# FFN 2's gate and up by 2x2 blocks with seven products, with one weight sum made in memory

## The reference

```
h = modulate(rms_norm(x, norm_ffn2), shift3, scale3)              # 512 x 1024
x = x + 0.5 * g3 * ((silu(h @ w_gate) * (h @ w_up)) @ w_down)     # w_gate, w_up: 1024 x 2816
```

## Time and profile before

| | |
|---|---|
| median of 3 runs | 1163.62 us (1163.49 to 1168.38) |
| the profiled execution | 1163.01 us |
| its span in the profile | 1161.2 us |
| mean granted clock of PE | 0.997 |
| PE busy | 1145.9 us, 99% of the span |
| DVE, ACT, POOL busy | 625.5, 451.7, 58.9 us |
| FFN 2's gate and up loop | 811.8 to 1029.4 us |

### The profile page before, as it was taken

How to read it: one execution, slowest core, us unless ns; L and a number is a source line. 1 busy time by engine, 2 the same in 40 slices (tenths; PEclk the granted TensorE clock), 3 DMA queues, 4 the chain that set the end, 5 groups by cost and what they waited for, 6 DMA issues and landing times.

```text
span 1161.2 us, 16214 instructions
## 1 busy us (share of the span) xinstructions
PE 1145.9 (99%) x5730; PEld 969.9 (84%) x5730; DVE 625.5 (54%) x1051; ACT 451.7 (39%) x709; POOL 58.9 (5%) x86
## 2 busy tenths in 40 slices
PE   8899999999999999999999999999999999999997
PEld 7788888888888998888888888899888888888887
DVE  5766666666555666776565566756433333333332
ACT  5233332332222357665555566434322222222232
POOL 3301000000000000010001010000000000000000
PEclk9999999999999999999999999999999999999999
DMA  9567566556555423343343442341333333333332
GB/s 312 162 219 243 181 218 204 174 184 211 172 172 167 110 63 102 91 125 86 90 120 96 111 117 72 91 139 37 97 98 101 90 98 101 90 93 94 99 113 74
DMA packets 221149, 151.45 MB, mean 130 GB/s; under 512 B 5078, under 2 KB 202916, under 8 KB 221108
## 3 DMA queue, kind: packets, MB, share of 16 engines
q1 hardware_dynamic: 217108, 138.76, 39.8%
q0 software_dynamic: 3280, 9.79, 3.2%
q10 hardware_dynamic: 720, 2.36, 0.6%
HBM read 148.73 MB, written 4.52 MB: 132 GB/s over the span
## 4 chain that ended last, share of the span: by engine, by line
PE 91%; DVE 2%; SPq 2%; issue 1%; DMA 1%; ACT 1%; POOL 0%; DVEq 0%; POOLq 0%; ACTq 0%
PE bank L1492 28%; PE bank L1494 28%; PE bank L1493 28%; PE bank L1827 2%; PE bank L1820 1%; SPq L446 1%; PE bank L1843 1%; PE bank L1815 1%; PE bank L1842 1%; DMA raw<-in_ffn_w_gate_dram 1%; SPq L465 1%; DMA adas<-in_ada_w_dram 1%; SPq L459 0%; DVE hL L1010 0%; DVE tmp L1005 0%
## 5 line engine op out<-in xcount | busy, mean ns | idle before, releaser
L1492 PE MATMUL bank<-hH,wH 128*128 128x512 f32 (+1 forms) x1072 | 413.2, 385 | 3.6 <-DVE hL L1010 3.1
L1494 PE MATMUL bank<-hH,wL 128*128 128x512 f32 (+1 forms) x1072 | 409.0, 382 | 0.0
L1493 PE MATMUL bank<-hL,wH 128*128 128x512 f32 (+1 forms) x1072 | 408.8, 381 | 0.0
L617 ACT ACTIVATE wH<-raw 128x1024 fp32r<-128x1024 f32 (+1 forms) x169 | 176.2, 1042 | 500.2 <-PE bank L1494 500.2
L944 DVE TENSOR_TENSOR wL<-raw,wH 128x1024 fp32r<-128x1024 f32 (+1 forms) x169 | 203.4, 1204 | 280.3 <-ACT wH L617 279.7
L1492 PEld LDWEIGHTS bank<-hH,wH 128*128 128x128 f32 x1072 | 201.6, 188 | 44.4 <-issue 5.1
L1494 PEld LDWEIGHTS bank<-hH,wL 128*128 128x128 f32 x1072 | 201.5, 188 | 39.1
L1493 PEld LDWEIGHTS bank<-hL,wH 128*128 128x128 f32 x1072 | 201.8, 188 | 37.7
L1492 PE MATMUL bank<-actH,wH 128*128 128x512 f32 (+1 forms) x332 | 126.9, 382 | 0.0
L1494 PE MATMUL bank<-actH,wL 128*128 128x512 f32 (+1 forms) x332 | 126.6, 381 | 0.0
L1493 PE MATMUL bank<-actL,wH 128*128 128x512 f32 (+1 forms) x332 | 126.6, 381 | 0.0
(11 more groups left out here) (204 smaller groups left out, 1188.6 us busy)
## 6 DMA issues: line engine op xcount, KB each, us to landing
adaw<-in_ada_w_dram SPq DMA_DIRECT2D x28, 1024.0 KB, 6.0
raw<-in_ffn_w_gate_dram SPq DMA_DIRECT2D x43, 512.0 KB, 3.8
raw<-in_ffn_w_up_dram SPq DMA_DIRECT2D x43, 512.0 KB, 3.8
raw<-in_mix_w_in_dram SPq DMA_DIRECT2D x41, 512.0 KB, 3.8
raw<-in_ffn_w_down_dram SPq DMA_DIRECT2D x32, 512.0 KB, 3.7
adas<-in_ada_w_dram SPq DMA_DIRECT2D x16, 512.0 KB, 8.2
raw<-in_ffn_w_down_dram SPq DMA_DIRECT2D x16, 384.0 KB, 3.4
raw<-in_mix_w_out_dram SPq DMA_DIRECT2D x8, 512.0 KB, 3.7
```

The costliest lines, as they stand in the source:

```text
L617: nc.scalar.activation(wH[s][:, :n * P], raw[s][:, :n * P], ACT.Copy).then_inc(hi_done, 1)
L1492: T.matmul(o, a[0], b[0], start=start, stop=False)
L1493: T.matmul(o, a[0], b[1], start=False, stop=False)
L1494: return T.matmul(o, a[1], b[0], start=False, stop=stop)
```

## The change

FF tiles are paired i with i + 11 (`HF` = 11). Pairs 0 and 1 are computed as before (eight units, the last four behind `to_ffn`). Pairs 2 to 10, nine of them, are computed as 2x2 blocks: the depth is cut into its two halves of 512 channels, the columns into tile i and tile i + 11, the tokens into two halves of 256. Such a product of 2x2 blocks takes seven block products in place of eight, each of a sum of weight blocks and a sum of token blocks. One product is 2 matrices x 4 depth tiles x 3 = 24 matmuls of 256 columns; gate and up stand side by side in one bank. The order of the products is 1, 2, 5, 6, 7, 3, 4.

- **Token sums**, once: POOL adds high and low halves of four blocks of h back together (`whole`), DVE makes four sums of them (`token_sums`), and ACT and DVE split these into high and low halves (`t_high`, `t_low`) for products 6, 7, 4 and 5. Products 1, 2 and 3 take blocks of h itself.
- **Weight sums**, for each pair: products 1, 2 and 4 take raw weights. Product 5's sum lies ready in memory (`wsum_d`): POOL issues eight transfers from memory to memory while FFN 1's down runs, and eight that add, one behind each pair's biases in the mixing (704 KB each). DVE makes the others: to 5's sum it adds 1's raw weights in place for 6 and then 2's for 3 (`next_r`), and 1's to the loaded block for 7 (`next_q`).
- **Loads**: five per pair in place of four, each two transfers of 256 KB, into four raw slots used in turn. A slot is free when the last sum or low half that reads it is done.
- **Weight halves**: seven per pair (`w_high` on ACT, `w_low` on DVE) with three slots, two products ahead of PE.
- **Results**: ACT copies the banks of products 1 and 5 out, DVE makes seven sums of 128x512 (`block`); ACT takes Silu of the gate's half, DVE multiplies (`multiply`), ACT and DVE split as before, for two tiles at once.
- **Down**: its first two units' weights go into the token sums' place, and SP loads them after the last `w_low`; the first unit waits for the tiles of eight pairs, the second for all 22.
- The stage is written out on all engines and not in a loop. Three semaphores of the table are merged to one (`table_moved`).

The diff, cut to its core:

```diff
+    ORDER_P = (1, 2, 5, 6, 7, 3, 4)
+    B_P = {1: 4, 2: 7, 5: 5, 6: 6, 7: 0, 3: 1, 4: 2}
...
+    LOADS = (1, 2, 5, 7, 4)
+    PACKET, SUM_ROWS = 4 * P, D // 2 // P
+    N_LOAD, W_SLOTS, RAW_SLOTS = len(LOADS), 3, 4
...
+        def load_of(n):
+            t, p = n // N_BL, ORDER_P[n % N_BL]
+            return N_LOAD * t + LOADS.index(5 if p in (6, 3) else p)
...
+                if l < 2:
+                    sp.wait_ge(lo_done, U_DN2 - 1 + l + FREE)
+                elif l == 2:
+                    sp.wait_ge(t_lo, 3)
+                elif l >= RAW_SLOTS:
+                    t0, p0 = (l - RAW_SLOTS) // N_LOAD, LOADS[(l - RAW_SLOTS) % N_LOAD]
+                    if p0 in (1, 2):
+                        sp.wait_ge(r_made, 2 * t0 + p0)
+                    if p0 == 1:
+                        sp.wait_ge(q_made, t0 + 1)
+                    elif p0 != 2:
+                        sp.wait_ge(w_lo, N_BL * t0 + ORDER_P.index(3 if p0 == 5 else p0) + 1)
+                for m in range(2):
+                    if p == 5:
+                        src = wsum_d[m].rearrange("(k p) n -> p k n", p=P)[:, :, i * P:(i + 1) * P]
+                    else:
+                        k0, tile = {1: (0, i), 2: (DT // 2, i), 4: (DT // 2, i + HF), 7: (0, i + HF)}[p]
+                        src = tiles_of(ws[m], slice(tile * P, (tile + 1) * P), DT // 2, k0)
+                    sp.dma_start(raw_slot(l)[:, m, :].rearrange("p (k n) -> p k n", k=DT // 2), src
+                                 ).then_inc(w_in[l % RAW_SLOTS], 16)
+            for i in range(DT // 2):
+                for k in range(6):
+                    k0, n = PARTS[k % 3]
+                    if i == 0 and k < 2:
+                        sp.wait_ge(w_lo, N_PROD)
+                    t = 2 * i + k // 3
+                    sp_load(sp, U_DN2, 6, i, k, tiles_of(ffn2_w_down, slice(t * P, (t + 1) * P), n, k0))
...
+            def weight_sum(step):
+                kind, row = step // SUM_ROWS, step % SUM_ROWS * P
+                m = kind % 2
+                w = (ffn2_w_gate, ffn2_w_up)[m]
+                to = wsum_d[m, row:row + P, :]
+                if kind < 2:
+                    pool.dma_start(to, w[0, row:row + P, HF * P:], max_dma_last_dim=PACKET).then_inc(w_summed, 16)
+                else:
+                    pool.wait_ge(w_summed, 16 * 2 * SUM_ROWS)
+                    pool.dma_start(to, w[0, D // 2 + row:D // 2 + row + P, HF * P:], accum_op=ALU.add,
+                                   max_dma_last_dim=PACKET).then_inc(w_summed, 16)
...
+            def w_high(n):
+                l, p = load_of(n), ORDER_P[n % N_BL]
+                if p in (6, 3):
+                    act.wait_ge(r_made, 2 * (n // N_BL) + 1 + (p == 3))
+                elif p == 7:
+                    act.wait_ge(q_made, n // N_BL + 1)
+                else:
+                    act.wait_ge(w_in[l % RAW_SLOTS], 32 * (l // RAW_SLOTS + 1))
+                if n < 2:
+                    act.wait_ge(unit_done, U_DN2 - 1 + n)
+                elif n >= W_SLOTS:
+                    act.wait_ge(p_done, n - W_SLOTS + 1)
+                nc.scalar.activation(by_two(w_slot(n)[0]), raw_slot(l), ACT.Copy).then_inc(w_hi, 1)
...
+            def two_by_blocks(t):
+                for at in range(N_BL):
+                    n = N_BL * t + at
+                    if n + 2 < N_PROD:
+                        w_high(n + 2)
+                    else:
+                        k = n + 2 - N_PROD
+                        act.wait_ge(p_done, N_PROD - N_BL + 4 + k)
+                        prep_home(U_DN2 + k, U_DN2)
+                    if t and at == 1:
+                        gates(t - 1, 1)
+                    if t and at in (2, 3):
+                        act_high(t - 1, at - 2)
+                    if at == 1:
+                        act.wait_ge(p_done, n)
+                        if t:
+                            act.wait_ge(multiplied, 2 * t - 1)
+                        nc.scalar.activation(K_P1, bank[:, B_P[1], :], ACT.Copy).then_inc(kept, 1)
+                    if at == 3:
+                        act.wait_ge(p_done, n)
+                        if t:
+                            act.wait_ge(multiplied, 2 * t)
+                        nc.scalar.activation(K_P5, bank[:, B_P[5], :], ACT.Copy).then_inc(kept, 1)
+                    if at == 6:
+                        gates(t, 0)
...
+            def next_r(t, q):
+                n, r = N_BL * t + 2 + q, raw_slot(N_LOAD * t + 2)
+                dve.wait_ge(w_lo, n + 1)
+                V.tensor_tensor(r, r, raw_slot(N_LOAD * t + q), ALU.add).then_inc(r_made, 1)
+            def next_q(t):
+                l = N_LOAD * t + LOADS.index(7)
+                dve.wait_ge(w_in[l % RAW_SLOTS], 32 * (l // RAW_SLOTS + 1))
+                V.tensor_tensor(raw_slot(l), raw_slot(l), raw_slot(N_LOAD * t), ALU.add).then_inc(q_made, 1)
...
+            def block(t, step):
+                to, a, b, copies, made, products = (
+                    (K_U2, K_P1, bank[:, B_P[6], :], 1, 0, 4), (K_P1, K_P1, bank[:, B_P[2], :], 1, 1, 2),
+                    (K_U3, K_U2, bank[:, B_P[7], :], 1, 1, 5), (K_U2, K_U2, K_P5, 2, 3, 0),
+                    (K_U2, K_U2, bank[:, B_P[3], :], 2, 4, 6), (K_P5, K_U3, K_P5, 2, 4, 0),
+                    (K_U3, K_U3, bank[:, B_P[4], :], 2, 6, 7))[step]
...
+            def two_by_blocks(t):
+                for at in range(N_BL):
+                    n = N_BL * t + at
+                    if n + 2 < N_PROD:
+                        w_low(n + 2)
+                    else:
+                        prep_home(U_DN2 + n + 2 - N_PROD)
+                    if at < 2:
+                        next_r(t, at)
+                    if at == 1:
+                        next_q(t)
+                    if t and at == 0:
+                        block(t - 1, 6)
+                        multiply(t - 1, 0)
+                    if t and at == 2:
+                        multiply(t - 1, 1)
+                        act_low(t - 1, 0)
+                    if t and at == 3:
+                        act_low(t - 1, 1)
+                    for step in {4: (0, 1), 5: (2, 3), 6: (4, 5)}[at] if at >= 4 else ():
+                        block(t, step)
...
+            def gate_up_by_blocks():
+                u0 = U_GU2
...
+                for n in range(N_PROD):
+                    t, p = n // N_BL, ORDER_P[n % N_BL]
+                    if t and p in (1, 5):
+                        pe.wait_ge(kept, 2 * t - 1 + p // 5)
+                    elif t:
+                        pe.wait_ge(c_made, 7 * t - 7 + {6: 1, 2: 2, 7: 3, 3: 5, 4: 7}[p])
+                    elif p in (7, 4):
+                        pe.wait_ge(silu_done[1][B_P[p] // 2], DIRECT + START)
+                    elif p == 3:
+                        pe.wait_ge(prod_done[1][0], DIRECT + START)
+                    if t == 0 and p in (5, 6, 7, 4):
...
                         pe.wait_ge(lo_done, u + 1 + FREE)
```

More of the change, by code:

```diff
@@ L348, in hybrid_block @@
         out_sent = sem("out_sent")
+        w_summed = sem("w_summed")
+        w_in = [sem(f"w_in{q}") for q in range(RAW_SLOTS)]
+        r_made = sem("r_made")
+        q_made = sem("q_made")
+        w_hi = sem("w_hi")
+        w_lo = sem("w_lo")
+        p_done = sem("p_done")
+        h_whole = sem("h_whole")
+        t_sum = sem("t_sum")
+        t_hi = sem("t_hi")
+        t_lo = sem("t_lo")
+        kept = sem("kept")
+        c_made = sem("c_made")
+        gated = sem("gated")
+        multiplied = sem("multiplied")
         def head_rows(h):
@@ L585, in _ @@
                     pool.dma_start(modrows, mod_d.rearrange("a (r n) -> (a r) n", n=P)).then_inc(modrows_in, 16)
+                    for step in range(2 * SUM_ROWS):
+                        pool.wait_ge(unit_done, U_DN1 + 2 + 2 * step)
+                        weight_sum(step)
                 if n == 2:
@@ L599, in _ @@
                         biases_a(i)
+                        weight_sum(2 * SUM_ROWS + PAIRS - 1 + i)
+                    weight_sum(2 * SUM_ROWS + 2 * PAIRS - 1)
+                if n == 4:
+                    pool.wait_ge(hL_done, 5 * DT)
+                    for q in range(4):
+                        whole(q)
         @block.scalar
@@ new lines, in t_high, with act_high, gates @@
+            def t_high(p, sums):
+                act.wait_ge(t_sum, sums)
+                nc.scalar.activation(moving(p)[0], hB[{6: 22, 7: 12, 4: 21, 5: 11}[p]][:, :, :], ACT.Copy).then_inc(t_hi, 1)
+            def act_high(t, j):
+                act.wait_ge(multiplied, 2 * t + 1 + j)
+                nc.scalar.activation(actH[:, DIRECT + t + HF * j, :], sg[:, j, :], ACT.Copy).then_inc(actH_done[1], 1)
+            def gates(t, j):
+                act.wait_ge(c_made, 7 * t + (5, 7)[j])
+                act.wait_ge(actL_done[1], 2 * (DIRECT + t) + START)
+                nc.scalar.activation(by_halves(sg[:, j, :]), of_gate((c1, c2)[j]), ACT.Silu, scale=(1.0, -1.0)[j]).then_inc(gated, 1)
```

(82 more changed lines are left out.)

154 lines of the change are left out of this document (136 added, 18 removed).

## The result

The changed kernel takes 1167.4 us in the median of 20 runs (1165.0 to 1171.6), the kernel before 1163.7 us beside it (1162.9 to 1168.8). The ratio is 1.0027 with a 95% interval of 1.0015 to 1.0039: no change by the 0.5% that the prediction set, and a small loss if anything. The forecast was 1164 us, no change. The profiled execution took a span of 1165.5 us, where the one before took 1161.2.

A forecast was written before the change was run, and what follows sets the result against it. DVE's chain with three hops to ACT was taken to bound the pairs at 21.06 us. +2.7 (first) - 7 x 0.70 + 1.1 (ninth) + 1.8 (into down) = +0.7: 1164 us, no change, range 1155 to 1174.

The forecast's parts named there:

- The rival of PE as the bound: FFN 2 pairs: DVE and ACT keep ahead, pairs come 20.02 us apart, -7.6 us, 1156 us; chance 0.12.
- The period: Steady pairs in FFN 2 come 21.06 us apart, set by DVE with three hops to ACT, against 21.76 before.
- rival 2: Each pair waits for product 4's raw weights landing late: +5.8 at 4.7 us, +9 at 5.0, +19 at 6.0; chance 0.15.
- the ruler: DVE's written order through one pair, timed from 0 at the low half of product 5's weights; next pair at 21.06.
- First pair and end: FFN 2's first pair takes 24.5 us (+2.7), the ninth 22.86, and the way into down costs another 1.8.
- the three waits: First pair: PE waits for products 5, 6 and 7, late by 1.8, 0.8 and 1.9 us.
- the two around the first down unit: PE waits 1.8 us for the late first down weights, then another 1.8 before the second down unit.
- Sum and total: Whole kernel: first pair, seven pairs, ninth pair and way into down sum to +0.7 us; median 1164.3.
- Elsewhere nothing: Outside FFN 2's changed stage, transfers for the sum in memory hide in FFN 1's down and mixing: cost 0, range 0 to +15.
- Rivals 3 and 5: DVE 3 to 5% slower when busier, 1170 us, chance 0.10; chained DVE starts cost nothing, 1161 us, chance 0.05.
- rival 3: DVE 3 to 5% slower than when a third busy: +5 to +8, 1170 us; chance 0.10.
- a period of 20.5: Steady pairs if the skill's rule held and chained DVE starts cost nothing extra; sum about -3 us.

The follow-up runs named there:

- second profile: The changed kernel, unchanged, profiled in another execution: 1165.7 us in one run.
- all four moves: Changed kernel plus late gate Silu, early sum for product 7, exchanged raw buffers and early product in the first pair: 1149.5 us, 0.9867 against the kernel before.

## Why the prediction held

**What bounds it.** Right: DVE's chain with its hops to ACT, not load and not PE. The rival of PE as the bound (0.12) was wrong for this order of the jobs and right for another: one move of a Silu brings it.

**The period.** 21.06 forecast, 21.13 and 21.20 measured. It is made of two kinds of pairs. In the first profile six of eight come 20.7 to 21.1 us apart, two 21.6 (893.75 to 915.37 above); in the second five come 20.9 to 21.0 apart and three 21.3 to 21.9. In the long ones it is a load, not the one that the prediction feared (product 4's, rival 2) but the next pair's product 2. Its split in a short and in a long pair, each with the issue of its second transfer ahead of it:

```profile
875.43 0.51 SPq L559 DMA_DIRECT2D act_both<-in_ffn_w_up_dram  x1
...
878.90 1.06 ACT L871 ACTIVATE wH<-act_both 128x1024 fp32r<-128x1024 f32 x1 [1.44 <-DMA act_both<-in_ffn_w_up_dram]
...
896.39 0.51 SPq L559 DMA_DIRECT2D raw<-in_ffn_w_up_dram  x1
...
901.08 1.06 ACT L871 ACTIVATE wH<-raw 128x1024 fp32r<-128x1024 f32 x1 [2.65 <-DMA raw<-in_ffn_w_up_dram]
```

3.4 us to land in the short pair and 4.7 in the long one. In the short pair DVE takes the low half up without a wait, in the long one it waits for this split. That was not on the ruler: it had the load whose slot comes free last and not the ones that SP issues behind it.

So part of the agreement is luck. In the short pair the chain alone takes 20.95 us, 0.11 less than forecast: product 4's low half starts 12.44 us into the ruler (863.07 to 875.51) and not at 12.65, since the load put there is not what it waits for, and the block sums take 0.10 more. The late loads then put 0.2 us back in the mean. In the first long pair DVE also stands idle for 0.47 us ahead of a block sum, with nothing in the profile that it waits for; that gap stands at the same block sum of the third pair in every profile of a changed kernel. The load alone would have made that pair as long; where the gap comes from is open.

```profile
863.07 1.23 DVE L1433 TENSOR_TENSOR wL<-act_both,wH 128x1024 fp32r<-128x1024 f32 x1 [1.04 <-ACT wH L871]
...
875.51 1.22 DVE L1433 TENSOR_TENSOR wL<-raw,wH 128x1024 fp32r<-128x1024 f32 x1
...
898.76 0.69 DVE L1487 TENSOR_TENSOR work<-work,bank 128x512 f32<-128x512 f32 x1 [0.47 <-issue]
...
902.17 1.23 DVE L1433 TENSOR_TENSOR wL<-raw,wH 128x1024 fp32r<-128x1024 f32 x1 [0.19 <-ACT wH L871]
```

**First pair and end.** 24.5 and 22.86 forecast, 24.3 and 23.0 measured; the three waits were put at 1.8, 0.8 and 1.9 and came at 1.6, 0.7 and 1.8; the two around the first down unit, 1.8 each, at 2.0 and, in the second profile, 1.5. What failed here is small: the second down unit takes 5.90 instead of 5.44. Of the 0.46, 0.20 is only where the part ends: ACT's split comes 0.20 us behind the start of PE's next unit, and the two direct units, which begin with such a split, are shorter for the same reason. PE's own unit takes 5.70:

```profile
1038.81 0.50 PE L1894 MATMUL bank<-actH,tH 128*128 128x512 f32 x1
1039.15 0.39 PE L1895 MATMUL bank<-actL,tH 128*128 128x512 f32 x1
...
1044.51 0.40 PE L1894 MATMUL bank<-actH,wH 128*128 128x512 f32 x1
```

The first start to the next is 0.34 instead of 0.23, which is 0.11; the other 0.15 is a slower beat of 0.233 through the whole unit. The wait is not its reason, since the first down unit of the version with all four moves, which nothing waits for, takes 5.57 (1020.31 to 1025.88). Why these two units are slower is open; the forecast had nothing for it.

**Sum and total.** +0.7 forecast, +1.3 and +1.8 measured: the period gave 0.5 to 1.0, the second down unit 0.26, and 0.1 less came in the first pair, the ninth and the first down unit together. The forecast median of 1164.3 was 3.1 us low: 0.6 to 1.1 of that is here. From the first norm of the mixing to the stage the two kernels differ by only 0.2, so the rest should lie ahead of that norm, which the prediction took as fixed. In the first profile of each kernel it does: of the 2.7 us there, 1.8 arose in the first 67 us and 0.9 in the rest of FFN 1, where PE waits for the small transfer. For the medians that is argued and not shown. The one slip in the sums is rival 2's: a landing of 6.0 us is 1.85 above the 4.15 on the ruler, nine times that and 0.7 is +17, not +19.

**Elsewhere nothing.** Right, shown by the kernel without the transfers. Inside it one size was off: GpSimd's four adds were put at 2.5 us each and take 2.86 (the first row below); they end at 819.57 and DVE asks for them at 822.57, so they are covered. Its issue of an adding transfer, put at 0.7 us, takes 1.9.

```profile
808.12 11.45 POOL L710 TENSOR_TENSOR hB<-hH,hL 128x1024 f32<-128x1024 f32 x4 [11.50 <-DVE hL L1277]
...
876.65 1.46 DVE L1487 TENSOR_TENSOR work<-work,bank 128x512 f32<-128x512 f32 x2
```

**Rivals 3 and 5.** DVE's 1024-element jobs take 1.22 us at 84% load, so rival 3 falls. Two chained 512-element jobs (the second waits until the first is done) take 1.46 us together (the second row, block sums), 0.77 from start to start, where unchained ones start 0.60 apart. The Trainium skill, VectorE: DVE Perf Modes, section "The DRAIN you can't avoid", says that a semaphore after each operation costs nothing extra, and would have them alike; the row decides, and a period of 20.5 was not seen.

## What to carry to other kernels

Here, trading matmuls for VectorE work moved the bound to the longest round trip between engines, not to the busiest one: VectorE stood at 84% and still held TensorE back. Lay the written order on a ruler with the durations of the profile, and look for each place where an engine asks another for something that it could have asked for one job sooner; here one such move gave 7.6 us of stage time and another 11.1. Check every load whose buffer comes free late, and the ones issued behind it.

## What was not expected of the hardware

- The granted clock fell inside the changed kernel's stage, right after PE's 2.0 us wait, to near its 1.2 GHz level:

```profile
1032.00:1034.00 2.00, 2.00 (x8) 1.52 (x7) 1.90 (x4) 0.00 (x0) 0.00 (x0) 0.62 0.59 173
1034.00:1036.00 2.00, 2.00 (x6) 1.60 (x5) 1.91 (x4) 0.63 (x1) 0.00 (x0) 0.53 0.49 128
```

  It cost nothing: the second down unit waits for DVE until then anyway (7.20 us from unit to unit here, 7.19 in the second profile, where the same wait was followed by a clock of 1.00).
- An adding transfer of 704 KB holds GpSimd for 1.9 to 2.0 us at its issue (once 2.7) and lands after 9.4 us in the median; a plain one holds it for 1.1 and lands after 6.2.
- The first two down units of the changed kernels have their matmuls 0.233 us apart, with or without a wait ahead, where the kernel before has 0.227 in the same units.
